# Moving the weights, the activations and the shared area of a two-model float32 kernel to a multiple of 512 bytes in SBUF

## The chip, the cores and the metric

The kernel runs on one core of a Trainium2 chip. The metric is the device time of one execution, in microseconds (us). It is given as the median of several executions, and one more execution was taken with a profile.

## What is computed

The input is a sequence of 512 tokens of width 1024 in float32. It passes two models, one after the other. The first has two layers: the mixer of layer 0 is a gated short convolution beside a state-space scan in chunks, the mixer of layer 1 is causal attention with forget gates, and each layer ends in a layer norm, a feed-forward part with a causal convolution, and a second layer norm. The second model is one layer with two mixers side by side, differential attention and block-sparse attention with compressed keys, merged by gates, and then a feed-forward part with a squared ReLU.

```python
def conv_ffn(x, w_up, conv_w, conv_b, w_down):
    h = causal_dwconv(x @ w_up, conv_w, conv_b)
    u, g = _split(h, [D_FF, D_FF])
    return (u * jax.nn.silu(g)) @ w_down

for i in range(DEPTH):
    mix = sconv_ssd_mixer(x, ...) if i % 2 == 0 else fox_mixer(x, ...)
    x = layer_norm(ALPHA * x + mix, ln_mix_g[i], ln_mix_b[i])
    x = layer_norm(ALPHA * x + conv_ffn(x, ...), ln_ffn_g[i], ln_ffn_b[i])
```

For the change it matters only that nearly all the work is products of a 512 by K activation with a K by N weight matrix.

## The kernel before

**Products in three terms.** Float32 accuracy is reached with the type float32r, which the kernel uses as a faster and coarser format: each weight and each activation is split into a high part (the value rounded by a copy to float32r) and a low part (the value minus the high part). A product is three matmuls into the same PSUM bank: high by high, high by low, low by high. The helper `mm3` (lines 152 to 159) issues them. With weights stationary (the first operand of `pe.matmul` after the output) it is lines 157, 158 and 159 that run, where the moving operand is 512 columns of an activation. With activations stationary it is lines 154, 155 and 156, where 512 columns of a weight move. In the profile's names the moving operand comes first: `PS<-XH,WH` has XH moving and WH stationary.

**The ring of weights.** SyncE streams all weights as units of 512 KB into RAW, a ring of two slots of 128 by 1024. ScalarE rounds a slot into WH (line 145), VectorE subtracts into WL (line 150), TensorE uses the unit in 24 matmuls and then counts `unit_done`, which frees WH for the unit two further on. RAW is free for its next load when VectorE's subtraction is done. The list STREAM sets the order of the units.

**Loops of TensorE.** `unit_fm` runs eight k-tiles into one bank, each with another tile of the moving activation. `kmajor_pe` keeps the activation tile and goes through four banks. `unit_tm` and `last_down_pe` move a weight of 512 columns and go through four banks with four column blocks of the stationary activation. `unit_pair` and `unit_halves` are forms of `unit_fm` for the first units of a stage.

**Stages.** A list `plan` names for each stage what each engine runs. Between stages each engine drains and counts on a semaphore, and in most stages the next one is entered ahead, without waiting for the others.

**Place in SBUF.** The helper `place` (line 56) puts a tile at the cursor and moves the cursor on by its size, rounded up to 32 bytes. With `at=` it puts the tile at a given address and leaves the cursor. All addresses are bytes within a partition. The first address is the allocator's start rounded up to a multiple of 64, which comes to 16512, or 32 × 512 + 128. From there the order is RAW, WH, WL, X, XH, XL (lines 84 to 90, each a multiple of 8192 bytes), then the small tiles (lines 91 to 117), then the shared area, whose start is called `arena` (line 118). The helper `a_` (line 120) puts a tile at `arena` plus a given number of KB. Most of the activations lie in the shared area in turns, one stage after another: YH and YL (the mixer's result), FH and FL (feed-forward), OH and OL (attention), YDH, YDL, YNH and the YNL tiles (the second model's mixers), MXH and MXL (merged), MH and ML (the last feed-forward), and single-precision tiles such as PB. PN and PTN lie over XH and XL (lines 2634 and 2635).

| tiles | first address | past a multiple of 512 |
|---|---|---|
| RAW, WH, WL, X, XH, XL | 16512 and up, in multiples of 8192 from there | 128 |
| IDF (first small tile) | 90240 | 128 |
| shared area | 106272 | 288 |

The matmuls that read the shared area in three terms are those of the stages out0a and out0b (YH), down0 and down1 (FH), foxout (OH), gated (YDH), merge (YNH), out2 (MXH) and mdna (MH), all as moving operand, and mdnb (MH, stationary). All other units have XH and XL as the activation.

```python
    base = (nc.sbuf_base + 63) // 64 * 64
    cursor = [base]
    def place(name, shape, dt=F32, at=None):
        size = int(np.prod(shape[1:])) * (2 if dt == BF16 else 4)
        if at is None:
            at = cursor[0]
            cursor[0] += (size + 31) // 32 * 32
        return nc.alloc_sbuf_tensor_at(name, shape, dt, offset=at)
```

Of the kernel before, what the change touches and what calls it, by code (L numbers as in the profile page):

```python
# [22 lines left out]
F32, F32R, BF16 = mybir.dt.float32, mybir.dt.float32r, mybir.dt.bfloat16  # L23
# [4 lines left out]
P = 128  # L28
SEQ, DM = 512, 1024
NC_ = SEQ // P  # L30
KT = DM // P
# [3 lines left out]
HEADS, HD = 16, 64  # L35
# [8 lines left out]
NSA_G = 4  # L44
# [6 lines left out]
def build(nc, A, out):  # L51
    ctx = ExitStack()
# [9 lines that stand above are left out]
# [12 lines left out]
    def turn(sh_, **counts):  # L74
# [4 lines left out]
        for name, n in counts.items():  # L79
            so_far[name] += n  # L80
        return s


    RAW = place("RAW", [P, 2, 1024])
    WH = place("WH", [P, 2, 1024], F32R)
    WL = place("WL", [P, 2, 1024], F32R)
# [1 line left out]
    xh_at = cursor[0]  # L88
    XH = place("XH", [P, KT, SEQ], F32R)
    XL = place("XL", [P, KT, SEQ], F32R)  # L90
    IDF = place("IDF", [P, P])
    ONES = place("ONES", [P, P])
    IDB = place("IDB", [P, P], BF16)
    MROW = place("MROW", [P, P], BF16)
    MCOL = place("MCOL", [P, P], BF16)
    PCOL = place("PCOL", [P, 608])
    BCP = place("BCP", [P, 768])

    narrow1 = cursor[0]
    SW = [(place("SWH1", [P, KT, 32], F32R), place("SWL1", [P, KT, 32], F32R)),  # L100
          (place("SWH2", [P, KT, 48], F32R), place("SWL2", [P, KT, 48], F32R))]
    TINY = place("TINY", [P, 512])
    EPS = place("EPS", [P, 2])
    NM = place("NM", [P, 16])
    RS = place("RS", [P, 16])
    RW = place("RW", [P, 16])
    LAM = place("LAM", [P, 8])
    CW2 = [place("CW2K", [P, 2, HD], at=narrow1), place("CW2V", [P, 2, HD], at=narrow1 + 512)]
    CPOS = place("CPOS", [P, 2, 16], at=narrow1 + 1024)
    TABK = place("TABK", [P, 2, HD], at=narrow1 + 1152)  # L110
    gt_at = cursor[0]
    GT = place("GT", [P, NC_, 48])
    DEC = place("DEC", [P, 3, 64], at=gt_at)
    DCOL = place("DCOL", [P, KT])
    kcf_at = cursor[0]
    KCF = place("KCF", [P, NSA_G, 32])
    CPROW = place("CPROW", [32, P], at=kcf_at)
    arena = cursor[0]

    def a_(name, kb, shape, dt=F32):  # L120
# [19 lines left out]
    def hi(act, b, U, i, u):  # L140
# [3 lines left out]
        act.wait_ge(unit_done, b + u + 1 + U * i)  # L144
        act.activation(WH[:, slot, :], RAW[:, slot, :], ACT.Copy).then_inc(hi_ready, 1)  # L145

    def lo(dve, b, U, i, u):
        slot = u % 2
        dve.wait_ge(hi_ready, b + u + 3 + U * i)
        dve.tensor_tensor(WL[:, slot, :], RAW[:, slot, :], WH[:, slot, :], ALU.subtract).then_inc(lo_ready, 1)  # L150

# [29 lines left out]
    def early_hi(act, b, s):  # L181
        for u in range(2):
            act.wait_ge(raw_loaded[u], 16 * ((b + u) // 2 + 2))
            act.wait_ge(s.half, s.at.half + u + 1)
            act.activation(WH[:, u, 0:512], RAW[:, u, 0:512], ACT.Copy).then_inc(s.hi, 1)

    def rest_hi(act, b, u):
        act.wait_ge(unit_done, b + u + 1)
        act.activation(WH[:, u, 512:1024], RAW[:, u, 512:1024], ACT.Copy).then_inc(hi_ready, 1)

    def early_lo(dve, b, s):
        for u in range(2):
            dve.wait_ge(s.hi, s.at.hi + u + 1)
            dve.tensor_tensor(WL[:, u, 0:512], RAW[:, u, 0:512], WH[:, u, 0:512], ALU.subtract).then_inc(s.lo, 1)

    def rest_lo(dve, b, u):
        dve.wait_ge(hi_ready, b + u + 3)
        dve.tensor_tensor(WL[:, u, 512:1024], RAW[:, u, 512:1024], WH[:, u, 512:1024], ALU.subtract).then_inc(lo_ready, 1)

# [196 lines left out]
    def broadcast_dma(sp):  # L396
        for c, src, n in BCAST:
            sp.dma_start(BCP[:, c:c + n], src[0, :].partition_broadcast(P)).then_inc(su.bc, 16)

    def setup_pool(pool):  # L400
        pool.memset(IDF[:, :], 0.0)
        pool.memset(ONES[:, :], 1.0)
        pool.memset(IDB[:, :], 0.0)
        pool.memset(MROW[:, :], 0.0)
        pool.memset(MCOL[:, :], 0.0)
        pool.memset(EPS[:, 0:1], LN_EPS)
        pool.memset(EPS[:, 1:2], RMS_EPS)
        pool.drain().then_inc(su.zero, 1)
        pool.wait_ge(su.zero, 1)
        for m in (IDF, IDB):  # L410
            pool.affine_select(out=m[:, :], in_=m[:, :], compare_op=ALU.not_equal, fill=1.0,
                               base=0, pattern=[[-1, P]], channel_multiplier=1)
        pool.affine_select(out=MROW[:, :], in_=MROW[:, :], compare_op=ALU.is_ge, fill=MASKED,
                           base=0, pattern=[[-1, P]], channel_multiplier=1)
        pool.affine_select(out=MCOL[:, :], in_=MCOL[:, :], compare_op=ALU.is_ge, fill=MASKED,
                           base=0, pattern=[[1, P]], channel_multiplier=-1)
# [3 lines left out]
    def setup_pe(pe):  # L420
        pe.wait_ge(su.zero, 1)
        for _ in range(8):
            pe.matmul(PS[:, 1, 0:P], ONES[:, :], ONES[:, :], start=True, stop=True)
        pe.wait_ge(su.ident, 1)
# [4 lines left out]
    def turn_x(pe, f):  # L429
        if f >= 6:  # L430
            pe.wait_ge(su.evd if f == 6 else su.eva, 1)
        for c in range(NC_):
            last = pe.transpose(PS[:, 2 + f % 6, c * P:(c + 1) * P], XT[:, c, f * P:(f + 1) * P], IDF[:, :])
        last.then_inc(su.tr, 1)
# [53 lines left out]
    def params_pe(pe):  # L488
        pe.wait_ge(su.par, 16 * len(PARAM_ROWS))
        for g in range(5):  # L490
            last = pe.transpose(PS[:, 6 + g // 4, (g % 4) * P:(g % 4) * P + ROWS_OF[g]], PROW[0:ROWS_OF[g], g, :],
                                IDF[0:ROWS_OF[g], 0:ROWS_OF[g]])
        last.then_inc(su.tr, 1)

    def params_dve(dve):
        dve.wait_ge(su.tr, KT + 1)
        for g in range(5):
            dve.tensor_copy(PCOL[:, COL_OF[g]:COL_OF[g] + ROWS_OF[g]],
                            PS[:, 6 + g // 4, (g % 4) * P:(g % 4) * P + ROWS_OF[g]])
# [45 lines left out]
    def fold_pe(pe, bank, tile, ready, done, n=2):  # L545
        w = P // n
        for j in range(KT // n):
            ready(j)
            for hh in range(n):
                last = pe.matmul(PS[w * hh:w * hh + w, bank, :], ONES[:, 0:w], tile(n * j + hh), start=j == 0,  # L550
                                 stop=j == KT // n - 1)
# [6 lines left out]
    def ln_pe(pe, s):  # L558
# [4 lines left out]
        pe.wait_ge(s.ev, s.at.ev + 1)  # L563
        pe.matmul(PS[:, 1, :], ONES[:, :], LT[:, 2, :], start=True, stop=True).then_inc(s.mean, 1)
        ssq_pe(pe, s, 2)

    def ssq_pe(pe, s, nth=1, bufs=SQ):
# [3 lines left out]
        for c in range(NC_):  # L571
            last = pe.matmul(PS[:, 6, c:c + 1], LT[:, 2, c * P:(c + 1) * P], ONES[:, 0:1], start=True, stop=True)
        last.then_inc(s.var, 1)
        fill_pe(pe, 5)
        pe.wait_ge(s.dg, s.at.dg + 1)
        pe.matmul(PS[:, 7, :], ONES[:, :], LT[:, 4, :], start=True, stop=True).then_inc(s.bc, 1)
        fill_pe(pe, 8)
# [19 lines left out]
    def ln_act(act, s, g, b, split=True):  # L597
# [4 lines left out]
        if split:  # L602
            for m in range(KT):
                act.wait_ge(s.tmp, s.at.tmp + m + 1)
                act.activation(XH[:, m, :], LT[:, SQ[m % 4], :], ACT.Identity, bias=PCOL[:, b + m:b + m + 1],
                               scale=PCOL[:, g + m:g + m + 1]).then_inc(s.hi, 1)

    def rstd_dve(dve, s):
        dve.wait_ge(s.std, s.at.std + 1)
        dve.reciprocal(LT[:, 3, 4:4 + NC_], LT[:, 3, 0:NC_])  # L610
        dve.drain()
        dve.tensor_tensor(LT[:, 4, :].rearrange("p (c t) -> p c t", c=NC_), IDF[:, :].unsqueeze(1).to_broadcast([P, NC_, P]),
                          LT[:, 3, 4:4 + NC_].unsqueeze(2).to_broadcast([P, NC_, P]), ALU.mult).then_inc(s.dg, 1)
# [28 lines left out]
    def ln_pool(pool, s, g, b):  # L642
        for m in range(KT):
            pool.wait_ge(s.tmp, s.at.tmp + m + 1)
            pool.tensor_scalar(X[:, m, :], LT[:, SQ[m % 4], :], PCOL[:, g + m:g + m + 1], PCOL[:, b + m:b + m + 1],  # L645
                               ALU.mult, ALU.add).then_inc(s.px, 1)

    def rms_act(act, s, g, ready, bufs=SQ):
        square_act(act, s, ready, 1, 1, bufs)
        for m in range(KT):  # L650
            act.wait_ge(s.tmp, s.at.tmp + m + 1)
            act.activation(XH[:, m, :], LT[:, SQ[m % 4], :], ACT.Copy, scale=PCOL[:, g + m:g + m + 1]).then_inc(s.hi, 1)

    def rms_dve(dve, s, g, bank_ready=None, after_res=None):
# [6 lines left out]
        for m in range(KT + 2):  # L661
# [3 lines left out]
            if m >= 2:  # L665
                k = m - 2
                dve.wait_ge(s.hi, s.at.hi + k + 1)
                dve.scalar_tensor_tensor(out=XL[:, k, :], in0=LT[:, SQ[k % 4], :], scalar=PCOL[:, g + k:g + k + 1],
                                         in1=XH[:, k, :], op0=ALU.mult, op1=ALU.subtract).then_inc(s.xl, 1)
# [179 lines left out]
    def narrow_turn_pe(pe, s, bank, n, buf):  # L849
        pe.wait_ge(s.copied, s.at.copied + 1)  # L850
        for c in range(NC_):
            last = pe.transpose(PS[:, bank + 1, c * n:(c + 1) * n], buf[0:n, c * P:(c + 1) * P], IDF[0:n, 0:n])
        return last
# [34 lines left out]
    def xbc_pe(pe):  # L888
        for n in range(12):
# [9 lines left out]
            if n == 2:  # L899
                pe.wait_ge(su.sw, 4)  # L900
                narrow_fm_pe(pe, nr[0], 4, SW[0], 0, 16)
            if n == 3:
# [13 lines left out]
    def xbc_act(act):  # L916
        early_hi(act, first["xbc"], ex)
        for n in range(13):
# [11 lines left out]
            if n == 4:  # L930
# [3 lines left out]
                act.activation(E_, E_, ACT.Exp, scale=-1.0)  # L934
                act.activation(BCP[:, 752:768], BCP[:, B_ALOG:B_ALOG + 16], ACT.Exp)
                act.drain().then_inc(sd.w, 1)
# [115 lines left out]
    def mixer_pe(pe):  # L1052
        for n in range(N_GATE + N_Z + N_OUT):
# [31 lines left out]
            if 8 <= n < 24 and n % 2 == 0:  # L1085
# [11 lines left out]
                for hh in range(2):  # L1097
                    for c in range(NC_):
                        pe.matmul(PS[:, 3 + hh, c * P:(c + 1) * P], IDB[:, :], MCOL[:, :], start=False,
                                  stop=c == NC_ - 1)  # L1100
# [318 lines left out]
    def pair_scores_pe(pe, s, t, sub, query, key, bias=None):  # L1419
        if 3 * t + sub >= 2:  # L1420
            pe.wait_ge(s.ex, s.at.ex + 3 * t + sub - 1)
        for hh in range(2):
            for k, (qb, c0) in enumerate(SUBS[sub]):
                pe.matmul(pair_score(t, sub, hh, c0 + qb * P, P), IDB[:, :], MROW[:, :],
                          start=k == 0, stop=False, skip_group_check=True)
# [1697 lines left out]
```

## Time and profile before

| | |
|---|---|
| median of 3 executions | 2629.14 us (2625.03 to 2636.7) |
| profiled execution, its own time | 2629.51 us |
| its span, first to last instruction | 2627.7 us |
| mean granted clock of TensorE | 0.989 of 2.4 GHz |
| matmuls in the trace | 12200 |
| VectorE busy, ScalarE busy | 1373.9 us, 982.4 us |
| DMA | 206.62 MB, 79 GB/s on average |

The profile lists for each engine the time in which it was busy, and groups of instructions by source line. Durations of matmuls overlap each other: the next one starts while the last is still running through the array. So the distance from one start to the next counts, not the duration. Lines that stand in a helper (such as 157) collect the matmuls of all stages, and the tile names tell them apart.

### The profile page before, as it was taken

The numbers are of one execution on the slowest core, as the hardware profiler recorded it, in microseconds if no ns is written. First come the engines' busy times: TensorE is split into PE (matmuls) and PEld (weight loads), VectorE is DVE, ScalarE is ACT, GpSimd is POOL, SyncE is SP. The second block draws the span as 40 slices with busy tenths as digits, with TensorE's granted clock in tenths as the row PEclk, the third lists the DMA queues.
The fourth block names the chain that finished last, engine by engine and source line by source line (L and its number), as shares of the span: only waits on it lengthen the run. The fifth ranks groups of instructions, "written<-read, shape, count | busy, mean of one in ns | idle before, by whom it ended". The sixth has DMA issues, their size and how long they took to land. (4 is left out here: it accounts for less than half of the span.)

```text
span 2627.7 us, 34010 instructions
## 1 busy us (share of the span) xinstructions
PE 2535.7 (96%) x12200; PEld 1979.4 (75%) x12200; DVE 1373.9 (52%) x1975; ACT 982.4 (37%) x1727; POOL 188.0 (7%) x338
## 2 busy tenths in 40 slices
PE   8999999999999999999999899899998999999999
PEld 7777776888786876688878587678886667778777
DVE  6655426777324344577742567745555654542532
ACT  4333424333213254433321334624344652431331
POOL 0000001000001022100000100300101540000000
PEclk9999999999999999999999999999999999999999
DMA  4222222333222320233322132042222003323232
GB/s 128 82 72 72 81 90 70 96 96 96 90 93 62 90 65 17 64 97 98 98 91 96 45 97 89 1 138 78 73 81 57 1 1 96 89 89 95 80 96 96
DMA packets 277343, 206.62 MB, mean 79 GB/s; under 512 B 12100, under 2 KB 233969, under 8 KB 277233
## 3 DMA queue, kind: packets, MB, share of 16 engines
q1 hardware_dynamic: 270465, 198.64, 25.7%
q10 hardware_dynamic: 6768, 6.51, 0.8%
q8 instruction: 70, 1.15, 0.2%
q14 instruction: 40, 0.33, 0.0%
HBM read 203.02 MB, written 2.10 MB: 78 GB/s over the span
## 5 line engine op out<-in xcount | busy, mean ns | idle before, releaser
L150 DVE TENSOR_TENSOR WL<-RAW,WH 128x1024 fp32r<-128x1024 f32 x362 | 443.5, 1225 | 876.7 <-ACT WH L145 870.6
L145 ACT ACTIVATE WH<-RAW 128x1024 fp32r<-128x1024 f32 x362 | 383.1, 1058 | 1134.5 <-PE PS L159 876.5
L157 PE MATMUL PS<-XH,WH 128*128 128x512 f32 x1568 | 619.8, 395 | 10.9 <-DVE LT L2779 4.0
L158 PE MATMUL PS<-XL,WH 128*128 128x512 f32 x1568 | 612.6, 391 | 0.0
L159 PE MATMUL PS<-XH,WL 128*128 128x512 f32 x1568 | 612.5, 391 | 0.0
L157 PEld LDWEIGHTS PS<-XH,WH 128*128 128x128 f32 x1568 | 296.0, 189 | 77.5 <-issue 10.9
L159 PEld LDWEIGHTS PS<-XH,WL 128*128 128x128 f32 x1568 | 295.7, 189 | 62.9
L158 PEld LDWEIGHTS PS<-XL,WH 128*128 128x128 f32 x1568 | 296.1, 189 | 60.7 <-issue 1.0
L154 PE MATMUL PS<-WH,XH 128*128 128x512 f32 x416 | 164.6, 396 | 4.6 <-DVE CPOS L2547 2.7
L156 PE MATMUL PS<-WL,XH 128*128 128x512 f32 x416 | 162.7, 391 | 0.0
L155 PE MATMUL PS<-WH,XL 128*128 128x512 f32 x416 | 162.6, 391 | 0.0
L157 PE MATMUL PS<-FH,WH 128*128 (+1 forms) x352 | 139.8, 397 | 3.3 <-ACT UP L774 3.3
L159 PE MATMUL PS<-FH,WL 128*128 (+1 forms) x352 | 139.5, 396 | 0.0
L158 PE MATMUL PS<-FL,WH 128*128 (+1 forms) x352 | 139.5, 396 | 0.0
L645 POOL TENSOR_SCALAR X<-LT,PCOL 128x512 f32<-128x512 f32 x32 | 32.9, 1034 | 1224.8 <-DVE LT L635 1224.0
L1535 DVE TENSOR_REDUCE NM<-PS 128x2 f32<-128x1024 f32 (+3 forms) x128 | 101.6, 817 | 13.3 <-PE PS L1435 12.8
L154 PEld LDWEIGHTS PS<-WH,XH 128*128 128x128 f32 x416 | 78.4, 188 | 23.4 <-DVE WL L150 3.7
L1585 POOL TENSOR_SCALAR PN<-PN,RW,GT 128x512 f32<-128x512 f32 (+3 forms) x128 | 76.2, 607 | 227.4 <-DVE RW L1545 227.2
L156 PEld LDWEIGHTS PS<-WL,XH 128*128 128x128 f32 x416 | 78.5, 189 | 16.5
L155 PEld LDWEIGHTS PS<-WH,XL 128*128 128x128 f32 x416 | 78.6, 189 | 15.9
L157 PEld LDWEIGHTS PS<-FH,WH 128*128 128x128 f32 x352 | 66.3, 188 | 20.2 <-ACT UP L774 4.1
L778 ACT ACTIVATE UT<-UT 128x512 f32<-128x512 f32 x44 | 27.8, 632 | 138.3 <-DVE UT L805 138.3
(503 smaller groups left out, 3701.8 us busy)
## 6 DMA issues: line engine op xcount, KB each, us to landing
RAW<-in_ffn_w_up SPq DMA_DIRECT2D x88, 512.0 KB, 3.8
RAW<-in_w_in SPq DMA_DIRECT2D x60, 512.0 KB, 3.6
RAW<-in_ffn_w_down SPq DMA_DIRECT2D x44, 512.0 KB, 3.6
RAW<-in_sc_ssm_w_in SPq DMA_DIRECT2D x42, 512.0 KB, 3.8
RAW<-in_w_mlp_up SPq DMA_DIRECT2D x32, 512.0 KB, 4.0
RAW<-in_w_mlp_down SPq DMA_DIRECT2D x32, 512.0 KB, 3.7
RAW<-in_fox_w_in SPq DMA_DIRECT2D x24, 512.0 KB, 3.8
RAW<-in_sc_ssm_w_out SPq DMA_DIRECT2D x16, 512.0 KB, 3.7
```

The source lines that it names most:

```text
L145: act.activation(WH[:, slot, :], RAW[:, slot, :], ACT.Copy).then_inc(hi_ready, 1)
L150: dve.tensor_tensor(WL[:, slot, :], RAW[:, slot, :], WH[:, slot, :], ALU.subtract).then_inc(lo_ready, 1)
L154: pe.matmul(o, ah, wh, start=first, stop=False)
L155: pe.matmul(o, al, wh, start=False, stop=False)
L156: return pe.matmul(o, ah, wl, start=False, stop=last)
L157: pe.matmul(o, wh, ah, start=first, stop=False)
L158: pe.matmul(o, wh, al, start=False, stop=False)
L159: return pe.matmul(o, wl, ah, start=False, stop=last)
L645: pool.tensor_scalar(X[:, m, :], LT[:, SQ[m % 4], :], PCOL[:, g + m:g + m + 1], PCOL[:, b + m:b + m + 1], ALU.mult, ALU.add).then_inc(s.px, 1)
L778: act.activation(UT[:, u, :], UT[:, u, :], ACT.Silu).then_inc(s.silu, 1)
L1535: last = dve.tensor_reduce(NM[:, col:col + 2], PS[:, 2 * (i % 2):2 * (i % 2) + 2, c0:c0 + n], AX, ALU.max, negate=True)
L1585: pool.tensor_scalar(p, p, RW[:, col:col + 1], 1.0 if gate is None else gate(t, hh, qb), ALU.mult, ALU.mult)
```

## The change

The order of the tiles changes, and with it their addresses. No instruction, loop, wait or transfer is changed. The small tiles now come first. EPS, NM, RS, RW, LAM and DCOL take no room of their own any more: NM, RS, RW, LAM and DCOL lie in columns 192 to 255 of PCOL, and EPS in columns 704 and up of BCP, columns that nothing else uses. Then the cursor is rounded up to a multiple of 512, and RAW, WH, WL, X, XH, XL and the shared area follow.

| tiles | first address after | past a multiple of 512 |
|---|---|---|
| IDF (first small tile) | 16512 | 128 |
| SWH1 (narrow weights) | 23808 | 256, as before |
| RAW, WH, WL, X, XH, XL | 32256 and up | 0 |
| shared area | 105984 | 0 |

```diff
--- before.py
+++ after.py
@@ -81,6 +81,36 @@
         return s
 
 
+    IDF = place("IDF", [P, P])
+    ONES = place("ONES", [P, P])
+    IDB = place("IDB", [P, P], BF16)
+    MROW = place("MROW", [P, P], BF16)
+    MCOL = place("MCOL", [P, P], BF16)
+    spare = cursor[0] + 4 * 192
+    PCOL = place("PCOL", [P, 608])
+    spare_b = cursor[0] + 4 * 704
+    BCP = place("BCP", [P, 768])
+
+    narrow1 = cursor[0]
+    SW = [(place("SWH1", [P, KT, 32], F32R), place("SWL1", [P, KT, 32], F32R)),
+          (place("SWH2", [P, KT, 48], F32R), place("SWL2", [P, KT, 48], F32R))]
+    TINY = place("TINY", [P, 512])
+    EPS = place("EPS", [P, 2], at=spare_b)
+    NM = place("NM", [P, 16], at=spare)
+    RS = place("RS", [P, 16], at=spare + 64)
+    RW = place("RW", [P, 16], at=spare + 128)
+    LAM = place("LAM", [P, 8], at=spare + 192)
+    CW2 = [place("CW2K", [P, 2, HD], at=narrow1), place("CW2V", [P, 2, HD], at=narrow1 + 512)]
+    CPOS = place("CPOS", [P, 2, 16], at=narrow1 + 1024)
+    TABK = place("TABK", [P, 2, HD], at=narrow1 + 1152)
+    gt_at = cursor[0]
+    GT = place("GT", [P, NC_, 48])
+    DEC = place("DEC", [P, 3, 64], at=gt_at)
+    DCOL = place("DCOL", [P, KT], at=spare + 224)
+    kcf_at = cursor[0]
+    KCF = place("KCF", [P, NSA_G, 32])
+    CPROW = place("CPROW", [32, P], at=kcf_at)
+    cursor[0] = (cursor[0] + 511) // 512 * 512
     RAW = place("RAW", [P, 2, 1024])
     WH = place("WH", [P, 2, 1024], F32R)
     WL = place("WL", [P, 2, 1024], F32R)
@@ -88,33 +118,6 @@
     xh_at = cursor[0]
     XH = place("XH", [P, KT, SEQ], F32R)
     XL = place("XL", [P, KT, SEQ], F32R)
-    IDF = place("IDF", [P, P])
-    ONES = place("ONES", [P, P])
-    IDB = place("IDB", [P, P], BF16)
-    MROW = place("MROW", [P, P], BF16)
-    MCOL = place("MCOL", [P, P], BF16)
-    PCOL = place("PCOL", [P, 608])
-    BCP = place("BCP", [P, 768])
-
-    narrow1 = cursor[0]
-    SW = [(place("SWH1", [P, KT, 32], F32R), place("SWL1", [P, KT, 32], F32R)),
-          (place("SWH2", [P, KT, 48], F32R), place("SWL2", [P, KT, 48], F32R))]
-    TINY = place("TINY", [P, 512])
-    EPS = place("EPS", [P, 2])
-    NM = place("NM", [P, 16])
-    RS = place("RS", [P, 16])
-    RW = place("RW", [P, 16])
-    LAM = place("LAM", [P, 8])
-    CW2 = [place("CW2K", [P, 2, HD], at=narrow1), place("CW2V", [P, 2, HD], at=narrow1 + 512)]
-    CPOS = place("CPOS", [P, 2, 16], at=narrow1 + 1024)
-    TABK = place("TABK", [P, 2, HD], at=narrow1 + 1152)
-    gt_at = cursor[0]
-    GT = place("GT", [P, NC_, 48])
-    DEC = place("DEC", [P, 3, 64], at=gt_at)
-    DCOL = place("DCOL", [P, KT])
-    kcf_at = cursor[0]
-    KCF = place("KCF", [P, NSA_G, 32])
-    CPROW = place("CPROW", [32, P], at=kcf_at)
     arena = cursor[0]
 
     def a_(name, kb, shape, dt=F32):
```

## Rows read from the trace of the kernel before

**Rows 1.** The page: span, busy time, slices of PE, its clock.

```profile
span 2627.7 us, 34010 instructions
...
PE 2535.7 (96%) x12200; PEld 1979.4 (75%) x12200; DVE 1373.9 (52%) x1975; ACT 982.4 (37%) x1727; POOL 188.0 (7%) x338
...
PEclk9999999999999999999999999999999999999999
```

**Rows 2.** Windows: busy us by engine in three matmul stretches.

```profile
core 0: us, PE busy (x) PEld busy (x) DVE busy (x) ACT busy (x) POOL busy (x), PEclk, DMA share, GB/s
560.00:660.00 100.00, 100.00 (x443) 82.81 (x442) 71.34 (x93) 38.19 (x54) 0.00 (x0) 1.00 0.32 94
700.00:790.00 90.00, 90.00 (x386) 72.33 (x385) 19.60 (x16) 16.97 (x16) 0.00 (x0) 1.00 0.29 94
2545.00:2610.00 65.00, 65.00 (x281) 52.27 (x280) 14.69 (x12) 12.55 (x12) 0.00 (x0) 1.00 0.29 89
```

**Rows 3.** Groups by line, PE: xcount, busy us, mean ns, idle before.

```profile
L157 PE MATMUL PS<-XH,WH 128*128 128x512 f32 x1568 | 619.8, 395 | 10.9 <-DVE LT L2779 4.0 <-DVE XL L640 3.5 <-DVE WL L481 2.8
...
L154 PE MATMUL PS<-WH,XH 128*128 128x512 f32 x416 | 164.6, 396 | 4.6 <-DVE CPOS L2547 2.7 <-ACT KTF L1622 1.0 <-DVE XL L668 0.5
...
L157 PE MATMUL PS<-FH,WH 128*128 (+1 forms) x352 | 139.8, 397 | 3.3 <-ACT UP L774 3.3
...
L157 PE MATMUL PS<-YH,WH 128*128 128x512 f32 (+1 forms) x128 | 51.5, 402 | 2.0 <-ACT ZS L1207 1.9
L156 PE MATMUL PS<-WL,MH 128*128 128x512 f32 x128 | 51.1, 399 | 0.0
L157 PE MATMUL PS<-MH,WH 128*128 (+1 forms) x128 | 50.8, 397 | 1.6 <-ACT RL L2746 1.6
...
L157 PE MATMUL PS<-YDH,WH 128*128 128x512 f32 x64 | 25.6, 400 | 0.0
```

**Rows 4.** Source line 157, XH moving, 560 to 660 us.

```profile
L157 PE MATMUL PS<-XH,WH x147: 389/389/389, 560.1 to 659.4; 128*128 128x512 f32 x147
```

**Rows 5.** Source line 157, shared-area tiles moving, two windows.

```profile
L157 PE MATMUL PS<-FH,WH x128: 392/397/400, 700.3 to 789.5; 128*128 x121, 128*128 128x512 f32 x7
...
L157 PE MATMUL PS<-YNH,WH x57: 392/397/400, 2164.6 to 2204.0; 128*128 128x512 f32 x57
```

**Rows 6.** Source line 154, WH moving: stationary XH, then MH.

```profile
L154 PE MATMUL PS<-WH,XH x45: 389/389/389, 911.8 to 941.7; 128*128 128x512 f32 x45
...
L154 PE MATMUL PS<-WH,MH x94: 392/392/392, 2544.6 to 2609.7; 128*128 128x512 f32 x94
```

**Rows 7.** Source line 157, a unit after a turn, 2457.4 to 2462.6.

```profile
L157 PE MATMUL PS<-XH,WH x8: 389/391/476, 2457.3 to 2462.2; 128*128 128x512 f32 x8
```

**Rows 8.** Timeline of PE at half clock, and its window.

```profile
2440.91 0.63 PE L158 MATMUL PS<-XL,WH 128*128 128x512 f32 x1
2441.34 0.63 PE L159 MATMUL PS<-XH,WL 128*128 128x512 f32 x1
...
2438.50:2441.50 3.00, 3.00 (x9) 2.32 (x8) 2.90 (x5) 0.00 (x0) 0.00 (x0) 0.50 0.38 115
```

**Rows 9.** Groups by shape: transposes of fp32 blocks.

```profile
L1455 PE MATMUL PS<-IDF,PN 128*128 128x128 f32 x320 | 42.3, 279 | 1.4 <-DVE PTN L1565 1.4
...
L1455 PE MATMUL PS<-IDF,PB 128*128 128x128 f32 x160 | 21.3, 279 | 0.6 <-DVE PT L1565 0.6
```

**Rows 10.** The page: weight splits on DVE and ACT, RAW loads.

```profile
L150 DVE TENSOR_TENSOR WL<-RAW,WH 128x1024 fp32r<-128x1024 f32 x362 | 443.5, 1225 | 876.7 <-ACT WH L145 870.6
L145 ACT ACTIVATE WH<-RAW 128x1024 fp32r<-128x1024 f32 x362 | 383.1, 1058 | 1134.5 <-PE PS L159 876.5
...
RAW<-in_ffn_w_up SPq DMA_DIRECT2D x88, 512.0 KB, 3.8
```

**Rows 11.** Groups by shape, DVE: one subtraction in both regions.

```profile
L811 DVE TENSOR_TENSOR FL<-FY,FH 128x512 f32 x40 | 27.7, 693 | 37.5 <-ACT FH L780 37.5
...
L194 DVE TENSOR_TENSOR WL<-RAW,WH 128x512 fp32r<-128x512 f32 x8 | 5.2, 689 | 6.3 <-ACT WH L185 6.3
```

## The prediction, made before the change was run

> **What bounds the kernel now.** I read the page first [rows 1]. TensorE's matmuls are busy for 2535.7 of the 2627.7 us span, no other engine is above 52%, and the granted clock is at its upper level, 2.4 GHz, in all forty slices. So the time is the number of matmuls multiplied by the spacing of their starts, plus small gaps. The windows [rows 2] confirm it: in three long stretches the matmuls are busy for 100.0 of 100, 90.0 of 90 and 65.0 of 65 us, at a granted clock of 1.00, while VectorE and ScalarE are far from full.
>
> The durations of single matmuls overlap (389 ns long, one every 227 ns), so the groups by line [rows 3] serve only to count them. The spacing comes from the rows of one source line in one window: line 157 is every third matmul of `mm3`, so the time from first to last start, divided by the count less one and by three, is the spacing.
> - XH or XL moving, WH or WL stationary [rows 4]: (659.4 − 560.1)/146/3 = 226.7 ns.
> - A tile of the shared area moving [rows 5]: FH gives (789.5 − 700.3)/127/3 = 234.1 ns, YNH gives (2204.0 − 2164.6)/56/3 = 234.5 ns. I use 234.3.
> - WH moving [rows 6]: with XH stationary (941.7 − 911.8)/44/3 = 226.5 ns, with MH stationary (2609.7 − 2544.6)/93/3 = 233.3 ns.
>
> All have 512 columns, 128 stationary columns, the same type and the same clock. What differs is the address. RAW, WH, WL, X, XH and XL lie 128 bytes past a multiple of 512, the shared area 288 bytes past one, which is only a multiple of 32. Could the order of work be the cause instead? The two halves of [rows 6] have almost the same loop (`unit_tm`, `last_down_pe`: four banks in turn), and YNH in [rows 5] runs mostly in `unit_fm`, the very loop of [rows 4]. Each pair differs by 7 to 8 ns, so the loop is excluded and the place of the tile remains. Other engines' load is excluded too: in [rows 2] the stretch with the busier VectorE and ScalarE (71 and 38 of 100 us) is the one with the shorter spacing.
>
> **The change, part by part.** It adds and removes no instruction, wait or DMA; it moves addresses.
>
> (a) The shared area goes from 288 past a multiple of 512 to 0 past it. The matmuls that read it, from [rows 3], three lines to each row: moving operands FH 3×352 = 1056, YH 384, MH 384, YDH 192, and three more tile pairs (OH, MXH, YNH) of YDH's size, 576; together 2592. Stationary MH: 384. I take the spacing that they should reach from the nearest rows, those with both operands an exact multiple of 512 bytes apart, 226.7 ns [rows 4]. The gain is 2592 × 7.6 ns = 19.7 us and 384 × 6.6 ns = 2.5 us, 22.2 us in all. All of it is on the path, since TensorE doesn't pause there [rows 2]. Its bounds: nothing from below, and from above the full rate of (b).
>
> (b) WH, WL, X, XH and XL go from 128 past to 0 past. 3×1568 + 3×416 = 5952 matmuls [rows 3] read no tile of the shared area. No row shows a 512-column matmul with operands at 0 past. The bounds are taken from the nearest rows: at best the pure column rate. At the lower clock level of 1.2 GHz the starts lie 0.43 us apart [rows 8], half of that at 2.4 GHz is about 213 ns, so 13.4 ns less each, 80 us. At worst they fall to the spacing of [rows 5], 7.6 ns more each, 45 us. I take 0, the row that they are nearest to: the distance between moving and stationary tiles stays a multiple of 512, and 128 past was already a multiple of 128.
>
> (c) Is the remaining 13.4 ns above 213.3 an effect of place at all? After a short pause, a unit of eight triples takes 4.9 us over 21 spacings [rows 7], and with the first, 0.09 us longer, taken out that is 229 ns on average against 226.7 steady. So the spacing also depends on how weight loads and matmuls fall in time. That makes a second gain possible, not likely.
>
> (d) Matmuls that read single-precision blocks at half rate, and transposes: PN lies at 128 past, PB at 288 past, and both turn in 279 ns [rows 9]. Nothing gained or lost.
>
> (e) VectorE and ScalarE: the same subtraction is 693 ns in the shared area and 689 ns in the ring [rows 11]. At 4 ns for each, the some 100 such steps that lie in the serial chains of the four norms give under 0.5 us; counted as nothing. The rest hides under the matmuls.
>
> (f) The weight ring follows a faster TensorE: a slot needs a load of 3.8 us, a split of 1.06 us and a subtraction of 1.23 us [rows 10], 6.1 us for two units of 24 × 0.2267 = 5.4 us each, 10.9 us. If that cover were gone, each unit would wait for the rest; it isn't near. RAW's new address can change only the 3.8 us, which this slack covers.
>
> (g) The small tiles: EPS, NM, RS, RW, LAM and DCOL now share the unused columns of PCOL and BCP. They are read as scalars per partition by instructions that exist already. No cost, with the 0.5 us of (e) as the bound either way.
>
> **Sum.** The profiled execution took 2629.5 us for a span of 2627.7, and the median of the three runs is 2629.1, so the base is the same. 2629.5 − 22.2 = 2607.3 us.
>
> A page of the Trainium skill speaks against this. By "SBUF — State Buffer", in the note on SBUF cachelines, SBUF is read in lines of 16 bytes and only a crossing to a new line is paid for. Both 128 and 288 are multiples of 16, so by that rule both layouts cross the same number of lines, and the sum would be 2629.5. [Rows 4, 5] differ by 7.6 ns with the same number of such lines, so here the trace doesn't agree that this rule is the whole cost.
>
> **The rivals.**
>
> 1. Place isn't what slows the shared area, or alignment cures only a part. For it: the fast and slow rows differ in distance between operands as well as alignment, and [rows 7] shows a part in timing. Against it: the two controlled pairs. Time 2629.5 with nothing cured, 2618 with half. Chance 0.12.
>
> 2. The full gain: at 0 past, all 8928 matmuls reach the column rate. 5952 × 13.4 = 80 us, 2592 × 21.0 = 54 us, 384 × 20.0 = 8 us; 2629.5 − 142 = 2488 us. A smaller version, 2 to 4 ns less each beyond (a), gives 2571 to 2589. For it: the loss of 13.4 ns has no other explanation in the profile. Against it: between 128 and 0 no row says anything. Chance 0.11. The Trainium skill, "TensorE: Matmul & The Clock Gate", section "Back-to-back issue gap", gives a warm spacing of N/2.4 + 2.5 ns, 215.8 ns for 512 columns; by that estimate the time would be near 2509 us. No row here shows 215.8 for this type.
>
> 3. The other side: with both operands starting on the very boundary, the two read streams of TensorE, moving columns and weight load, meet in the same place more often, and the XH rows [rows 4] fall to the spacing of [rows 5]. 5952 × 7.6 = 45 us, with the shared area unchanged: 2675 us. It decides from 22.2/5952 = 3.7 ns more on each of those matmuls, if the shared area still gains. For it: [rows 7] shows that the same addresses run slower at another phase. Against it: these two tiles keep their distance to each other. Chance 0.09.
>
> **How the numbers follow.** A measurement of this kernel tells apart about 0.5%, 13 us. The forecast has 0.68 (2603 to 2611), rival 1 0.12, rival 2 0.11, rival 3 0.09. Faster by over 13 us: the forecast and rival 2, 0.79. Within: rival 1, 0.12. Slower: rival 3, 0.09. The range goes from 2588 (the small end of rival 2) to 2619 (a half cure), which leaves out the full gain, no effect and rival 3, about 2 in 10.
>
> **What would show it.** Right: FH, YNH and MH rows of the changed kernel at a steady 226.7 ns, line 157 with XH unchanged, PE busy about 22 us less, the same instruction count. The duration column should go from 397 to 389 ns in the shared-area groups. Wrong: FH still at 234 (rival 1), XH below 226 (rival 2) or above 230 (rival 3), or time lost in gaps of PE, which would point to the ring.

## The result and the profile after

The changed kernel takes 2609.57 us (median of 6, 2606.72 to 2614.82), the kernel before 2632.07 us (median of 6). The ratio on record is 0.992 with a 95% interval of 0.9904 to 0.9935: some 21 us faster. The medians themselves are 22.5 us apart. The forecast was 2607 us, in a range of 2588 to 2619.

The page after, with the rows that answer to [rows 1]:

```profile
span 2610.2 us, 34010 instructions
...
PE 2515.4 (96%) x12200; PEld 1977.0 (76%) x12200; DVE 1373.6 (53%) x1975; ACT 982.5 (38%) x1727; POOL 188.1 (7%) x338
...
PEclk9999999999999999999999999999999999999999
```

The same 34010 instructions and the same busy time of VectorE (1373.6 us), ScalarE and GpSimd; TensorE's own is 20.3 us less. All source lines are three higher than before, so line 157 is now 160 and line 154 is 157.

The groups by line, engine PE, against [rows 3]:

```profile
L160 PE MATMUL PS<-XH,WH 128*128 128x512 f32 x1568 | 619.0, 395 | 11.7 <-DVE LT L2782 4.0 <-DVE WL L484 3.7 <-DVE XL L643 3.5
...
L157 PE MATMUL PS<-WH,XH 128*128 128x512 f32 x416 | 165.9, 399 | 5.5 <-DVE CPOS L2550 2.7 <-DVE XL L671 1.5 <-ACT KTF L1625 1.0
...
L160 PE MATMUL PS<-FH,WH 128*128 (+1 forms) x352 | 137.2, 390 | 3.3 <-ACT UP L777 3.3
...
L160 PE MATMUL PS<-MH,WH 128*128 (+1 forms) x128 | 49.9, 390 | 1.6 <-ACT RL L2749 1.6
...
L159 PE MATMUL PS<-WL,MH 128*128 128x512 f32 x128 | 49.8, 389 | 0.0
...
L160 PE MATMUL PS<-YDH,WH 128*128 128x512 f32 x64 | 25.2, 393 | 0.0
```

FH fell from a mean duration of 397 to 390 ns, MH moving from 397 to 390, WL over MH from 399 to 390, YDH from 400 to 391. XH,WH stayed at 395. WH over XH rose from 396 to 399, though no distance of it changed: 7 of these matmuls in place of 3 are followed by a start 0.4 to 0.5 us later, the distance at the lower clock level. These durations overlap, so the spacing must again come from first and last start. Starts are printed to 0.1 us, which leaves some 0.3 ns of doubt on a spacing over 100 triples and some 0.8 ns over 44, so 226.4 and 226.8 are the same here. One source line in one window each, for XH moving, FH moving, YNH moving and WH moving over a stationary MH, against [rows 4 to 6]:

```profile
L160 PE MATMUL PS<-XH,WH x148: 389/389/389, 554.9 to 654.9; 128*128 128x512 f32 x148
...
L160 PE MATMUL PS<-FH,WH x126: 389/389/389, 699.7 to 784.7; 128*128 x118, 128*128 128x512 f32 x8
...
L160 PE MATMUL PS<-YNH,WH x57: 389/389/468, 2151.3 to 2189.4; 128*128 128x512 f32 x57
...
L157 PE MATMUL PS<-WH,MH x96: 389/389/389, 2530.1 to 2594.7; 128*128 128x512 f32 x96
```

(654.9 − 554.9)/147/3 = 226.8 ns for XH, (784.7 − 699.7)/125/3 = 226.7 ns for FH, (2189.4 − 2151.3)/56/3 = 226.8 ns for YNH, (2594.7 − 2530.1)/95/3 = 226.7 ns for MH. The second column tells the same in another way: smallest, median and largest duration of FH are now all 389 ns, where they were 392, 397 and 400 [rows 5]. Each matmul is now like the next.

The ring, against [rows 10], is unchanged but for 0.1 us of a load, which nothing waits for:

```profile
L153 DVE TENSOR_TENSOR WL<-RAW,WH 128x1024 fp32r<-128x1024 f32 x362 | 443.6, 1225 | 860.7 <-ACT WH L148 854.7
L148 ACT ACTIVATE WH<-RAW 128x1024 fp32r<-128x1024 f32 x362 | 383.1, 1058 | 1117.2 <-PE PS L162 858.2
...
RAW<-in_ffn_w_up SPq DMA_DIRECT2D x88, 512.0 KB, 3.7
```

The span of the traced execution fell by 17.5 us only (2627.7 to 2610.2), where the counts give 22.2. The query for spans and the mean granted clock says why. Before:

```profile
core 0: 2627.7 us, clock 0.989
```

After:

```profile
core 0: 2610.2 us, clock 0.987
```

After, once more, in an execution of the run `after_again` (below):

```profile
core 0: 2605.3 us, clock 0.989
```

A mean clock of 0.987 in place of 0.989 is 0.002 × 2 × 2610 = 10 us more at the lower of the two levels, where work takes about twice as long ([rows 8]: 0.43 us from start to start), so 5 us lost. At the same clock as before the span is 2605.3 us, 22.4 us less. The mean clock differs as much between executions of one kernel: 0.986 to 0.991 in the six of the changed kernel, 0.984 to 0.991 in those of the kernel before. So no part of this difference is put down to the change.

### The profile page after: what moved, and what is told of

Same layout as the page of the kernel before. It is cut to its first block and busy times, and to the rows that moved or that the text cites. A ratio compares the mean times of both kernels' runs of the same rounds, so it can differ in the third digit from the quotient of the medians.

```text
span 2610.2 us, 34010 instructions
## 1 busy us (share of the span) xinstructions
PE 2515.4 (96%) x12200; PEld 1977.0 (76%) x12200; DVE 1373.6 (53%) x1975; ACT 982.5 (38%) x1727; POOL 188.1 (7%) x338
## 5 line engine op out<-in xcount | busy, mean ns | idle before, releaser
L160 PEld LDWEIGHTS PS<-FH,WH 128*128 128x128 f32 x352 | 66.1, 188 | 17.5 <-ACT UP L777 4.1
```

The source lines that it names most:

```text
L160: pe.matmul(o, wh, ah, start=first, stop=False)
```

## The experiments

All are edits of the changed kernel, except for one that is an edit of the kernel before. They move addresses; only one (`narrow`) changes the work. In the notation below D is the address of the moving tile minus that of the stationary tile, modulo 256. The line numbers differ by one or two between kernels, as the edits add lines.

### Does each tile's own place count, or the distance between two?

```diff
     cursor[0] = (cursor[0] + 511) // 512 * 512
+    cursor[0] += 128        # all128;  32 in all32
     RAW = place("RAW", [P, 2, 1024])
```

> RAW, WH, WL, X, XH, XL and the shared area all 128 bytes past a multiple of 512, the rest as in the changed kernel. Theory D (what counts is the distance between the moving and the stationary tile) and theory A (each of the two must lie at a multiple of 64 or 128 for itself): FH, YNH and MH rows stay at 226.7 ns, time about 2610 us. Rival 512 (only a multiple of 512 cures): the shared-area rows leave 226.7 ns and the time rises towards 2630 us.

Measured: 2611.48 us (2606.99 to 2614.64), ratio to before 0.9917 (0.9891 to 0.9943). FH moving:

```profile
L161 PE MATMUL PS<-FH,WH x126: 389/389/389, 699.8 to 784.8; 128*128 x117, 128*128 128x512 f32 x9
```

(784.8 − 699.8)/125/3 = 226.7 ns. A multiple of 512 isn't needed.

> The same tiles all 32 bytes past a multiple of 512, so every distance stays a multiple of 512. Theory D: nothing changes, 226.7 ns everywhere, about 2610 us. Theory A: every 512-column matmul in three terms is slow, 234 ns or more also with XH moving; 8928 matmuls by 7.6 ns are 68 us, so about 2678 us.

Measured: 2611.06 us (2609.82 to 2611.67), ratio 0.9921 (0.9896 to 0.9945). XH moving, then FH moving:

```profile
L161 PE MATMUL PS<-XH,WH x148: 389/389/389, 554.9 to 654.8; 128*128 128x512 f32 x148
...
L161 PE MATMUL PS<-FH,WH x125: 389/389/389, 700.3 to 784.6; 128*128 x116, 128*128 128x512 f32 x9
```

(654.8 − 554.9)/147/3 = 226.5 and (784.6 − 700.3)/124/3 = 226.6 ns. With every operand at 32 past a multiple of 512, as badly placed by itself as the shared area of the kernel before, nothing is lost. Theory A falls, theory D stands.

### The shared area alone, and the weights alone, at 32 past

```diff
-    arena = cursor[0]
+    arena = cursor[0] + 32
```

> Only the shared area moves, to 32 past a multiple of 512; the ring and XH stay at 0. Both theories: the shared-area rows go back to about 234.3 ns (moving) and 233.3 ns (stationary MH), XH rows stay at 226.7 ns; 22 us more, about 2632 us. If it stays near 2610, the loss of the kernel before came from the residue 288 rather than from being off a multiple of 64.

Measured: 2628.49 us (2623.68 to 2633.56), ratio 0.9986 (0.9971 to 1.0). FH moving, then WH moving over MH:

```profile
L160 PE MATMUL PS<-FH,WH x122: 393/395/397, 700.1 to 784.8; 128*128 x119, 128*128 128x512 f32 x3
...
L157 PE MATMUL PS<-WH,MH x86: 395/396/396, 2539.9 to 2599.4; 128*128 128x512 f32 x86
```

(784.8 − 700.1)/121/3 = 233.3 ns with D = 32, (2599.4 − 2539.9)/85/3 = 233.3 ns with D = 224. The gain is gone, with the ring and XH still at a multiple of 512. The moving row came out 1 ns below the 234.3 expected, which has a meaning below: the size of the loss depends on D.

```diff
     cursor[0] = (cursor[0] + 511) // 512 * 512
+    cursor[0] += 32
     RAW = place("RAW", [P, 2, 1024])
     WH = place("WH", [P, 2, 1024], F32R)
     WL = place("WL", [P, 2, 1024], F32R)
+    cursor[0] += 96
     X = place("X", [P, KT, SEQ])
```

> RAW, WH and WL at 32 past a multiple of 512, X, XH, XL and the shared area at 128 past: now all pairs are off, the weights alone being badly placed. Theory D and A: all 8928 matmuls slow, by 6.6 to 7.6 ns, 59 to 68 us, about 2669 to 2678 us. If only the moving operand counts, the rows with XH or FH moving stay at 226.7 ns, only those with WH moving slow down (1248 + 384, by 7 ns 11 us), about 2621 us.

Measured: 2662.63 us (2656.84 to 2666.52), ratio 1.011 (1.0082 to 1.0138), so clearly slower than the kernel before; 53 us above the changed kernel. XH moving, FH moving, WH moving over MH:

```profile
L162 PE MATMUL PS<-XH,WH x143: 392/392/392, 560.0 to 659.4; 128*128 128x512 f32 x143
...
L162 PE MATMUL PS<-FH,WH x115: 399/399/399, 709.6 to 789.4; 128*128 x115
...
L159 PE MATMUL PS<-WH,MH x72: 392/397/497, 2570.0 to 2620.0; 128*128 128x512 f32 x72
```

(659.4 − 560.0)/142/3 = 233.3 ns, (789.4 − 709.6)/114/3 = 233.3 ns, and (2620.0 − 2570.0)/71/3 = 234.7 ns, 234.3 without the first matmul's 0.1 us. So a badly placed stationary tile slows a well placed moving one: it isn't the moving operand alone. The time is 6 to 15 us under what I expected. Only the smaller step of 6.6 ns applies to most matmuls, which is the 59 us of the lower end. The missing 6 us may lie in units that start after a pause and were above 226.7 ns already [rows 7]; that isn't shown.

### How coarse is the distance?

The shared area moves by 64, 128 and 256, by the edit of `arena32` with another number.

> Only the shared area moves, to 64 past a multiple of 512. Theory D64 (only the distance modulo 64 counts): shared-area rows stay at 226.7 ns, about 2610 us. Theory D128 or coarser: they rise to 231 to 234 ns, 13 to 22 us more, 2623 to 2632 us. A spacing under 226.7 ns would show that a distance of 0 isn't the best one.

Measured: 2616.78 us (2615.1 to 2619.3), ratio 0.9943 (0.9924 to 0.9963). FH moving (D = 64), WH moving over MH (D = 192):

```profile
L160 PE MATMUL PS<-FH,WH x125: 387/388/389, 699.8 to 784.9; 128*128 x118, 128*128 128x512 f32 x7
...
L157 PE MATMUL PS<-WH,MH x86: 392/396/399, 2540.0 to 2599.5; 128*128 128x512 f32 x86
```

(784.9 − 699.8)/124/3 = 228.8 ns and (2599.5 − 2540.0)/85/3 = 233.3 ns. The two aren't the same, though both are off by 64: the sign of the distance seems to count. The 64 was measured with the activation moving and the 192 with the weight moving, in another loop; at 0, 96, 128 and 160, which were measured both ways, the two ways agree within 0.7 ns, so the loop isn't a likely cause. Theory D64 falls, and its alternative, 231 to 234 ns for all rows, was too high for FH.

> Shared area at 128 past. Theories D64 and D128: shared-area rows at 226.7 ns, about 2610 us. Theory D256 or D512: slower rows, up to 234 ns, up to 2632 us.

Measured: 2626.69 us (2622.13 to 2629.74), ratio 0.9979 (0.9965 to 0.9994). The same two rows, D = 128 in both:

```profile
L160 PE MATMUL PS<-FH,WH x123: 390/393/405, 699.8 to 784.9; 128*128 x121, 128*128 128x512 f32 x2
...
L157 PE MATMUL PS<-WH,MH x87: 390/393/405, 2540.0 to 2599.9; 128*128 128x512 f32 x87
```

(784.9 − 699.8)/122/3 = 232.5 ns, (2599.9 − 2540.0)/86/3 = 232.2 ns. A shared area at a neat multiple of 128 is nearly as slow as that of the kernel before.

> Shared area at 256 past. Theories D64, D128 and D256: 226.7 ns, about 2610 us. Theory D512: slower rows, up to 2632 us.

Measured: 2611.21 us (2607.19 to 2612.57), ratio 0.9917 (0.9887 to 0.9948). The same rows, D = 0 by modulo 256:

```profile
L160 PE MATMUL PS<-FH,WH x125: 389/389/389, 700.2 to 784.5; 128*128 x116, 128*128 128x512 f32 x9
...
L157 PE MATMUL PS<-WH,MH x88: 389/389/389, 2540.3 to 2599.4; 128*128 128x512 f32 x88
```

(784.5 − 700.2)/124/3 = 226.6 ns, (2599.4 − 2540.3)/87/3 = 226.4 ns. A distance of 256 is as good as 0 and one of 128 isn't, so the modulus is 256.

A shared area 16 bytes past a multiple of 512 was to be measured as well, with about 2630 us expected. It has no result, since a tile starts on a multiple of 32 bytes here, so nothing is known of smaller steps. With the rows above, all eight distances that a step of 32 bytes allows are measured:

| D, moving minus stationary, modulo 256 | spacing of starts, ns | from |
|---|---|---|
| 0 | 226.4 to 226.8 | after, all128, all32, arena256; before [rows 4] |
| 32 | 233.3 | arena32, FH moving |
| 64 | 228.8 | arena64, FH moving |
| 96 | 233.3 | w32, XH and FH moving; before, WH over MH [rows 6] (128 − 288) |
| 128 | 232.2 to 232.5 | arena128, both |
| 160 | 234.1 to 234.5 | before [rows 5] (288 − 128); w32, WH over MH |
| 192 | 233.3 | arena64, WH over MH |
| 224 | 233.3 | arena32, WH over MH |

Two entries are reached from different addresses in different kernels, 96 and 160, and agree. The table also gives the times: `arena128` should lose 2976 × 5.7 ns = 17 us against the changed kernel, and lost 17.1; `arena64` should lose 2592 × 2.1 + 384 × 6.6 ns = 8.0 us, and lost 7.2. Against `arena256`, which ran beside them on the same chip, they lost 15.5 and 5.6 us.

### The smallest edit that should do all of it

If only the distance counts, neither the new order nor the multiple of 512 is needed. In the kernel before, the shared area is 160 past a multiple of 256 as seen from WH and XH, so 96 bytes more bring it to 0.

```diff
--- before.py
-    arena = cursor[0]
+    arena = cursor[0] + 96
```

> The kernel before with one number changed: the shared area starts 96 bytes further on, at 106368, so that its distance to WH and XH is a multiple of 256; no other tile moves. Theory D256 (only the distance between moving and stationary tile modulo 256 counts): shared-area rows at 226.7 ns and the whole gain of the change, about 2610 us. Rival (the new order of the tiles, or the multiple of 512, has a part in the gain): between 2615 and 2630 us.

> The changed kernel once more beside the one above on the same chip: about 2610 us, and the same as it within 4 us by theory D256.

Measured, on the same chip and against the same runs of the kernel before: `minimal96` 2613.56 us (2607.75 to 2616.67), ratio 0.9935 (0.9915 to 0.9955); `after_again` 2612.42 us (2607.11 to 2613.17), ratio 0.9932 (0.9914 to 0.995). They differ by 1.1 us, less than either scatters. `minimal96`, XH moving, FH moving, WH over MH:

```profile
L157 PE MATMUL PS<-XH,WH x147: 389/389/389, 555.2 to 654.5; 128*128 128x512 f32 x147
...
L157 PE MATMUL PS<-FH,WH x126: 389/389/389, 699.9 to 784.9; 128*128 x117, 128*128 128x512 f32 x9
...
L154 PE MATMUL PS<-WH,MH x96: 389/389/389, 2530.2 to 2594.8; 128*128 128x512 f32 x96
```

99.3/146/3, 85.0/125/3 and 64.6/95/3 are 226.7 ns each. The whole gain of the change is in one number. The other moves are not needed for the time; no version ran that beats the changed kernel.

### Which stationary tile does the moving stream collide with?

TensorE loads the next stationary tile while the present matmul streams. WL moves behind XL, 32 bytes past a multiple of 512, so that in each triple with XH moving only one stationary tile is off. The shared area starts where WL ends and moves along: it is 32 from WH and 0 from WL.

```diff
     WH = place("WH", [P, 2, 1024], F32R)
-    WL = place("WL", [P, 2, 1024], F32R)
     X = place("X", [P, KT, SEQ])
     xh_at = cursor[0]
     XH = place("XH", [P, KT, SEQ], F32R)
     XL = place("XL", [P, KT, SEQ], F32R)
+    cursor[0] += 32         # wl32;  256 in wl256
+    WL = place("WL", [P, 2, 1024], F32R)
```

> WL alone moves behind XL, 32 bytes past a multiple of 512, and with it the shared area; RAW, WH, X, XH and XL stay at 0. With XH moving only the third matmul of each triple has a badly placed stationary tile. The profile shows each weight load start with the matmul before its own. Theory N (what collides is the moving stream with the load of the next weights): the spacing after the second matmul (XL moving, WL being loaded) is the long one, 233 against 227 ns. Theory O (the distance to its own stationary tile counts): the spacing after the third one. Either way XH rows average about 229 ns; the shared area is 32 from WH and 0 from WL, about 231 ns. Time about 2632 us (XH 4704 by 2.2 ns is 10 us, weights moving 1248 by 2.2 to 4.4 ns is 3 to 5 us, shared area 2592 by 4.4 ns is 11 us, MH 1 us, on top of 2608).

Measured: 2663.67 us in a single execution, where I expected 2632. The timeline shows the overlap: the load of line 163 (WL) starts within 0.01 us of the matmul of line 162 (XL moving, on WH).

```profile
600.09 0.40 PE L162 MATMUL PS<-XL,WH 128*128 128x512 f32 x1
600.10 0.19 PEld L163 LDWEIGHTS PS<-XH,WL 128*128 128x128 f32 x1
600.33 0.39 PE L163 MATMUL PS<-XH,WL 128*128 128x512 f32 x1
600.33 0.19 PEld L161 LDWEIGHTS PS<-XH,WH 128*128 128x128 f32 x1
```

The three terms with XH moving, in the order in which they run:

```profile
L161 PE MATMUL PS<-XH,WH x143: 395/395/395, 560.0 to 659.4; 128*128 128x512 f32 x143
L162 PE MATMUL PS<-XL,WH x143: 400/400/400, 560.2 to 659.6; 128*128 128x512 f32 x143
L163 PE MATMUL PS<-XH,WL x144: 389/389/389, 559.7 to 659.8; 128*128 128x512 f32 x144
```

A matmul's duration follows roughly its own spacing to the next start: before, the median is 389 ns at 226.7 [rows 4] and about 397 at 234.3 [rows 5]. The second term, beside which WL is loaded, is the longest (400 ns), the third, whose own stationary tile is the misplaced WL, the shortest (389 ns). That speaks for theory N and against theory O, but three things keep it from showing either. First, theory N as I wrote it had the other two at 227 ns (389 ns of duration), and the first term takes 395. Second, in `w32` all three distances are the same, 96, and the terms still differ by up to 7 ns. With XH moving the first term, shown above, takes 392 ns and the third is the longest; with FH moving the first is the longest, 399 ns, also shown above. The second and third terms of XH, then of FH, in `w32`:

```profile
L163 PE MATMUL PS<-XL,WH x143: 394/394/394, 560.3 to 659.7; 128*128 128x512 f32 x143
L164 PE MATMUL PS<-XH,WL x144: 399/399/399, 559.8 to 659.9; 128*128 128x512 f32 x144
...
L163 PE MATMUL PS<-FL,WH x115: 392/392/392, 709.9 to 789.7; 128*128 x115
L164 PE MATMUL PS<-FH,WL x115: 394/394/394, 710.1 to 789.9; 128*128 x115
```

Third, with FH moving in `wl32` only the distance to WL is good. Theory N would have the second term the shortest there, theory O the third, and it is the third:

```profile
L161 PE MATMUL PS<-FH,WH x114: 397/397/397, 710.3 to 789.4; 128*128 x114
L162 PE MATMUL PS<-FL,WH x115: 397/397/397, 709.8 to 789.6; 128*128 x115
L163 PE MATMUL PS<-FH,WL x115: 393/393/393, 710.0 to 789.8; 128*128 x115
```

So which of the two matmuls beside a load is the one that matters stays open. What the run does show is the average over a triple. XH moving averages (659.4 − 560.0)/142/3 = 233.3 ns and FH (789.4 − 710.3)/113/3 = 233.3 ns. One bad distance in three (XH) or two in three (FH) costs as much as three in three. The size of the expectation (2632 us) was wrong for this reason.

> Control of the kernel with WL moved by 32: WL again behind XL, but 256 bytes past a multiple of 512, and the shared area with it. Theory D256: all rows at 226.7 ns, about 2610 us. If the new order of the tiles itself had cost time there, XH rows would be at 229 ns or more here too, and the time above 2630 us.

Measured: 2609.91 us in a single execution.

```profile
L161 PE MATMUL PS<-XH,WH x147: 388/389/390, 560.1 to 659.4; 128*128 128x512 f32 x147
...
L161 PE MATMUL PS<-FH,WH x125: 388/389/390, 700.0 to 784.4; 128*128 x115, 128*128 128x512 f32 x10
```

(659.4 − 560.1)/146/3 = 226.7 and (784.4 − 700.0)/124/3 = 226.9 ns. The order of the tiles itself costs nothing, so the 54 us between the two come from the 32 bytes, by which WL and the shared area are off together. The two are single executions on different chips. Their mean clocks are 0.986 and 0.987, and the step of 6.6 ns on each of the 8928 matmuls would be 59 us.

### The 13 ns that remain

```diff
-            last = mm3(pe, o, WH[:, slot, k * P:(k + 1) * P], WL[:, slot, k * P:(k + 1) * P],
+            last = mm3(pe, o, WH[:, slot, k * P:k * P + n], WL[:, slot, k * P:k * P + n],
```

Here n is 64 in mupa, 32 in mupb and 128 elsewhere (these are the two stages that apply the squared ReLU), and the output has n partitions: the kernel leaves out the rest of each output in these stages.

> The changed kernel, but in the two stages that apply the squared ReLU the stationary operand has 64 columns in the first (mupa) and 32 in the second (mupb) instead of 128; the upper part of each output is left out. 384 matmuls each, 512 columns moving as before, all distances a multiple of 256. Theory L (the 13.4 ns that remain above 213.3 come from the weight load reading beside the moving stream): the spacing falls with the width, to about 220 ns at 64 and 217 ns at 32 columns. Theory F (they are fixed for each matmul, or the load's width doesn't matter): 226.7 ns in both. Time 2610 us by F, 2604 us by L.

Measured: 2613.89 us in a single execution. The two stages, 64 columns and then 32, each with the same stretch of the changed kernel (128 columns) behind it:

```profile
L160 PE MATMUL PS<-XH,WH x87: 389/397/472, 2265.1 to 2324.5; 128*64 128x512 f32 x87
L160 PE MATMUL PS<-XH,WH x88: 389/389/475, 2265.3 to 2324.6; 128*128 128x512 f32 x88
...
L160 PE MATMUL PS<-XH,WH x45: 391/392/398, 2487.2 to 2517.8; 128*32 128x512 f32 x45
L160 PE MATMUL PS<-XH,WH x44: 389/389/389, 2486.7 to 2515.9; 128*128 128x512 f32 x44
```

(2324.5 − 2265.1)/86/3 = 230.2 ns and (2517.8 − 2487.2)/44/3 = 231.8 ns, against (2324.6 − 2265.3)/87/3 = 227.2 and (2515.9 − 2486.7)/43/3 = 226.4 ns. Both theories fail: with a narrower stationary tile the spacing is longer, not shorter, although D is still 0. The output is narrower too, and no run parts the two. The value 226.7 ns isn't a sum of a pure stream and a cost for each column loaded. What the 13.4 ns between it and 213.3, the 512 columns at 2.4 GHz, consist of stays open.

## Why the prediction was right, and where its reasons were not

**What bounds the kernel** held: TensorE's busy time fell by 20.3 us and the span with it, and nearly nothing of it was lost in gaps. TensorE's idle time rose from 92.0 to 94.8 us. The working read the digits of [rows 1] as the upper clock level in all forty slices. They say only 90% or more of it: [rows 8] is a stretch at the lower level, and the mean clock is 0.989.

**Part (a)**, the shared area, was predicted at 226.7 ns from the nearest rows and measured at 226.7; the term of 22.2 us agrees with the 22.4 us between two traces of the same mean clock and the 22.5 us between the medians, and the ratio on record gives 21 us. The pairs with nearly the same loop ([rows 4] against YNH in [rows 5], and the two halves of [rows 6]) were the step that carried it. They excluded the loop, but left open whether the place or the distance counts; this change cures both, so the number came right without that being known.

**Part (b)**, the ring and XH, was taken at 0 with bounds of −80 and +45 us, and is 0. The reason given first, that the distance between moving and stationary tile stays a multiple of 512, was the right one. The second, that 128 past is already a multiple of 128, was not: `all32` shows that the place itself doesn't count, and `arena128` that a multiple of 128 isn't enough.

**Parts (d) to (g)** cost nothing, as assumed: VectorE's busy time is 1373.6 us after 1373.9. `minimal96`, which has none of the other moves, takes the same time.

**Part (c)** asked whether the rest above 213.3 ns is an effect of place. No row at any of eight distances is below 226 ns, so for these layouts it isn't; `narrow` leaves its nature open. The bound of 80 us was somewhat high: the 0.43 us of [rows 8] halves to 215 ns and not to 213, which makes it some 70 us.

**The rivals.** Rival 1 held that distance might matter beside alignment. The premise was right and its conclusion not: since the distance is what counts, the change cures all of it. Rival 2 (full column rate) didn't come. The formula of the Trainium skill, "TensorE: Matmul & The Clock Gate", section "Back-to-back issue gap", N/2.4 + 2.5 = 215.8 ns, is given there for an isolated matmul and not for a stream with weight loads. No stretch measured here meets it, the best being at 226.7. Rival 3 didn't come either, but the mechanism that it names is real in another form: `w32` made every pair bad and cost 53 us. It needed a change of the distance, and this change keeps that of the ring to XH.

**The rule on lines of 16 bytes** from the Trainium skill, "SBUF — State Buffer", note on SBUF cachelines, was weighed and set aside. The runs agree with setting it aside: 32, 64 and 128 are all multiples of 16 and cost 6.6, 2.1 and 5.7 ns. The same page of the Trainium skill says under "Who interferes with whom" that TensorE's two read ports are independent. In these runs the two reads aren't independent: the spacing depends on the distance between the moving and the stationary addresses, and the places that both were moved to together (`all128`, `all32`) changed nothing.

**What the working left out**: the time at the lower clock level differs by some 10 us between the two traces of the changed kernel, worth 5 us. Read from one pair of traces alone, the gain would have been 17.5 us.

## What to carry to other kernels

When TensorE is the bound, don't take the duration or spacing of a 512-column matmul as a constant: compute the spacing from first and last start of a line in a steady window, tile by tile, and compare tiles with the same loop. Where float32r operands of 512 columns stream in step with weight loads, put the moving and the stationary tiles a multiple of 256 bytes apart; in this kernel one bad area cost 22 us of 2632, and a misplaced weight tile together with the shared area behind it 54. Moving the start of an area by the missing bytes is enough, and a general alignment isn't required. All this was measured with float32r, 512 moving and 128 stationary columns; other types and widths weren't.

## What the runs showed of the hardware that was not expected

- The spacing of starts of float32r matmuls depends on the distance between moving and stationary addresses modulo 256, not on either address. It doesn't look symmetric: 228.8 ns at 64, 233.3 ns at 192, though in different loops.
- One bad distance in three is as dear as three in three (233.3 ns in `wl32` and in `w32`), which suggests, but doesn't show, that the two streams fall into step once and then stay in it, or never do. The single value 389 ns for smallest, median and largest duration at D = 0, against 392 to 400 at D = 160, fits this. So does the unit of [rows 7] (before, D = 0): its first nine spacings after the long one average (2459.72 − 2457.63)/9 = 232 ns, the next twelve (2462.44 − 2459.72)/12 = 226.7 ns. A single value isn't proof, though: `wl32` and `w32` have single values too, at 233.3 ns.

```profile
2457.63 0.40 PE L158 MATMUL PS<-XL,WH 128*128 128x512 f32 x1
...
2459.72 0.39 PE L158 MATMUL PS<-XL,WH 128*128 128x512 f32 x1
...
2462.44 0.39 PE L158 MATMUL PS<-XL,WH 128*128 128x512 f32 x1
```

- Narrower stationary tiles (with narrower outputs) at D = 0 lengthen the spacing, from 227.2 to 230.2 ns at 64 columns and from 226.4 to 231.8 ns at 32.
- The effect wasn't seen where fp32 blocks of 128 columns are transposed. IDF moves there and lies 128 past, so PN at 128 is at D = 0 and PB at 288 at D = 96, with the same mean duration of 279 ns [rows 9]. These are durations; the spacing wasn't worked out.
